# Sparse attention's pair loop: copies out of PSUM put ahead of ScalarE's other work in each step, one scaling moved a step on VectorE, one turning moved ahead on TensorE

## The reference, cut to what matters

```python
def nsa_attention(h, w_in, q_g, kc_g, ks_g, kw_g, pe_k, pe_v, ck_w1, ck_w2, cv_w1, cv_w2, w_out):
    q, kc, vc, ks, vs, kw, vw, gl = jnp.split(h @ w_in, splits, axis=-1)
    q = rmsnorm(heads(q, N_HEADS), q_g)
    q_nope = to_groups(q)
    q_rope = to_groups(partial_rope(q))
    gates = jax.nn.sigmoid(gl)
    k_cmp = rmsnorm(compress(kc_blk, pe_k, ck_w1, ck_w2), kc_g)      # 31 compressed keys
    v_cmp = compress(vc_blk, pe_v, cv_w1, cv_w2)
    ...
        p_c = masked_softmax(einsum(qn, k_cmp) * scale, cmp_end <= pos)
        o_c = einsum(p_c, v_cmp)
        p_s = masked_softmax(einsum(qr, k_g) * scale, mask_s)
        o_s = einsum(p_s, v_g)
        p_w = masked_softmax(einsum(qr, kwb) * scale, mask_w)
        o_w = einsum(p_w, vwb)
        return gt[..., 0:1] * o_c + gt[..., 1:2] * o_s + gt[..., 2:3] * o_w
    return o @ w_out
```

## Time and profile before

| what | value |
|---|---|
| time, median of 3 runs | 2884.02 us (2883.28 to 2886.16) |
| the profiled execution's own time | 2889.93 us |
| its span | 2888.1 us |
| mean granted clock of TensorE | 0.983 |
| PE, DVE, ACT busy | 96%, 57%, 41% of the span |
| NSA's pair loop | about 2237 to 2466 us of the span |
| length of a middle pair, from one start of L1017 to the next | 27.85 us (2286.81 to 2314.66) |

### The profile page before, as it was taken

How to read it: one execution, slowest core, us unless ns; L and a number is a source line. 1 busy time by engine, 2 the same in 40 slices (tenths; PEclk the granted TensorE clock), 3 DMA queues, 4 the chain that set the end, 5 groups by cost and what they waited for, 6 DMA issues and landing times.

```text
span 2888.1 us, 34237 instructions
## 1 busy us (share of the span) xinstructions
PE 2766.0 (96%) x11807; PEld 2092.8 (72%) x11807; DVE 1652.5 (57%) x2288; ACT 1196.0 (41%) x1929; POOL 151.1 (5%) x141
## 2 busy tenths in 40 slices
PE   8999998999989988999989989999997999999999
PEld 6777776888867656888866657888875555788887
DVE  4444426776254755777339955554375787555532
ACT  4333324444243544444236654333244566433321
POOL 0000000000000000000005710000000222000000
PEclk9999999999999999999999999999999999999999
DMA  4222232333322112333321213333333000233322
GB/s 144 76 78 73 73 95 67 100 89 94 95 71 88 52 39 71 95 94 92 92 77 52 66 44 88 94 94 93 91 102 104 15 16 23 73 94 94 94 88 94
DMA packets 419614, 229.26 MB, mean 79 GB/s; under 512 B 7939, under 2 KB 411468, under 8 KB 419404
## 3 DMA queue, kind: packets, MB, share of 16 engines
q1 hardware_dynamic: 418172, 225.18, 26.6%
q10 hardware_dynamic: 1360, 3.02, 0.3%
HBM read 226.07 MB, written 2.10 MB: 79 GB/s over the span
## 4 chain that ended last, share of the span: by engine, by line
PE 83%; DVE 9%; ACT 5%; issue 2%; DMA 1%; POOL 1%; DVEq 0%; ACTq 0%; POOLq 0%; SPq 0%
PE lin L725 21%; PE lin L727 21%; PE lin L726 21%; DVE con_a L2368 2%; PE stat L741 1%; DVE w_lo L1918 1%; PE lin L1025 1%; PE att L870 1%; PE att L834 1%; PE att L833 1%; PE att L835 1%; PE att L986 1%; ACT w_hi L1332 1%; ACT n_pt L1634 1%; PE lin L1048 1%
## 5 line engine op out<-in xcount | busy, mean ns | idle before, releaser
L1918 DVE TENSOR_TENSOR w_lo<-raw,w_hi 128x1024 fp32r<-128x1024 f32 x427 | 527.7, 1236 | 654.0 <-ACT w_hi L1332 639.5
L1332 ACT ACTIVATE w_hi<-raw 128x1024 fp32r<-128x1024 f32 x427 | 452.2, 1059 | 771.1 <-PE lin L727 678.9
L725 PE MATMUL lin<-xh,w_hi 128*128 128x512 f32 x1856 | 741.8, 400 | 4.4 <-DVE w_lo L1918 4.0
L727 PE MATMUL lin<-xh,w_lo 128*128 128x512 f32 x1856 | 733.7, 395 | 0.0
L726 PE MATMUL lin<-xl,w_hi 128*128 128x512 f32 x1856 | 733.7, 395 | 0.0
L725 PEld LDWEIGHTS lin<-xh,w_hi 128*128 128x128 f32 x1856 | 348.5, 188 | 97.0 <-issue 12.0
L726 PEld LDWEIGHTS lin<-xl,w_hi 128*128 128x128 f32 x1856 | 348.5, 188 | 86.9 <-issue 3.4
L727 PEld LDWEIGHTS lin<-xh,w_lo 128*128 128x128 f32 x1856 | 348.3, 188 | 85.3
L726 PE MATMUL lin<-ffn_lo,w_hi 128*128 128x512 f32 x704 | 279.1, 396 | 0.0
L725 PE MATMUL lin<-ffn_hi,w_hi 128*128 128x512 f32 x704 | 279.1, 396 | 0.0
L727 PE MATMUL lin<-ffn_hi,w_lo 128*128 128x512 f32 x704 | 279.1, 396 | 0.0
(11 more groups left out here) (365 smaller groups left out, 3801.8 us busy)
## 6 DMA issues: line engine op xcount, KB each, us to landing
raw<-in_ffn_w_up SPq DMA_DIRECT2D x176, 512.0 KB, 3.8
raw<-in_ffn_w_down SPq DMA_DIRECT2D x64, 512.0 KB, 3.6
raw<-in_a_w_in SPq DMA_DIRECT2D x48, 512.0 KB, 3.8
raw<-in_ffn_w_down SPq DMA_DIRECT2D x32, 384.0 KB, 3.1
raw<-in_conv_w_pw SPq DMA_DIRECT2D x24, 512.0 KB, 3.9
raw<-in_nsa_w_in SPq DMA_DIRECT2D x21, 512.0 KB, 3.8
raw<-in_a_w_out SPq DMA_DIRECT2D x16, 512.0 KB, 3.6
raw<-in_w_kv SPq DMA_DIRECT2D x16, 512.0 KB, 3.9
```

What stands on the lines that cost most here:

```text
L725: pe.matmul(bank, w_hi[s][:, k, :], h, start=start and k == 0, stop=False)
L727: done = pe.matmul(bank, w_lo[s][:, k, :], h, start=False, stop=stop and k == kc - 1)
L1332: act.activation(w_hi[s][:, :, :], raw[s][:, :, :], ACT.Copy).then_inc(hi_done[s], 1)
L1918: dve.tensor_tensor(w_lo[s][:, :, :], raw[s][:, :, :], w_hi[s][:, :, :].bitcast(F32), ALU.subtract).then_inc(lo_done[s], 1)
```

## The change

ScalarE: in every step `place(n)` comes directly behind `exps(n+1)`. It moves ahead of `high_out` in step 1, of `square` in step 2, of `inverse_rms` in step 3 (with the copy `pct`, which stays directly behind it), of `split_next` in step 5 and of `exp_compressed` in step 7. VectorE: `normed_q` moves from step 3 to step 4, directly ahead of `rotated_q`. TensorE: in step 4 `turn(n)` moves ahead of `weigh_compressed` and `weigh(p, 0)`. No instruction is added or taken away.

```diff
@@ TensorE, nsa @@
                         if i == 0 and p:
                             weigh(p - 1, 1, before)
+                        if i == 3 and not last_pair:
+                            head_sums(lin[ub])
+                        turn(n)
                         if i == 4:
                             weigh_compressed(p, own[0])
                             weigh(p, 0, own[0])
-                        if i == 3 and not last_pair:
-                            head_sums(lin[ub])
-                        turn(n)
@@ ScalarE, nsa @@
                             exps(n + 1)
+                        place(n)
                         if i == 1 and p:
                             high_out(p - 1, before)
+                        if i == 3:
+                            act.wait_ge(n_tc, p + 1)
+                            if p:
+                                act.wait_ge(n_pv, 2 * p - 1)
+                            act.activation(pct[:, :], lin[bo][0:2 * NCMP, :], ACT.Copy).then_inc(n_pc, 1)
                         if not last_pair:
...
                                 split_next()
                             if i == 7:
                                 exp_compressed(p + 1)
-                        place(n)
-                        if i == 3:
-                            act.wait_ge(n_tc, p + 1)
-                            if p:
-                                act.wait_ge(n_pv, 2 * p - 1)
-                            act.activation(pct[:, :], lin[bo][0:2 * NCMP, :], ACT.Copy).then_inc(n_pc, 1)
@@ VectorE, nsa @@
                         if not last_pair:
-                            if i == 3:
+                            if i == 4:
                                 normed_q(p + 1, b)
-                            if i == 4:
                                 rotated_q(p + 1)
```

## The result

The changed kernel takes 2908.11 us (median of 4 runs, 2906.65 to 2912.56), the kernel before 2884.13 us (4 runs): a ratio of 1.0083, with a 95% interval of 1.0071 to 1.0095. It is slower by 24.0 us. The direction was forecast, but 24.0 us is more than the 14.5 us predicted, and the time lies above the range. (In the profiles the spans differ by 22.7 us. The loop began 2.8 us later in the kernel before's, 2237.08 against 2234.26 us, which the change has no part in.)

What follows compares the result with a forecast made beforehand. TensorE, 83% of the chain, was taken as the bound, with a mid-pair relay between engines. Six pairs at 2.37 (14.2) + 0.6 first pair - 0.3 last pair = 14.5 us: 2884.0 to 2898.5, range 2890 to 2904.

Steps and rivals of the forecast that it cites:

- pct, turning and q scaling: Fourth and fifth steps: the 0.75 us wait for pct goes; the later q scaling makes the sixth turning wait 0.6.
- square: Behind the third step's copies: head sums 2.30 us late, only some 0.35 us of it on top of att_hi.
- w_hi: Behind the sixth step's copies: exponentials 2.35 us late, so the pair ends about 2.37 late instead of 2.15.
- att_hi: Behind the second step's copies: VectorE's att_lo waits for it, and TensorE's third turning gets 1.95 us of new wait.
- the relay: Engines handing work on mid-pair, TensorE hardly ahead: all moves together make pairs 1 to 6 each 2.37 us longer.
- The second rival: Relay slack absorbs part of the late start; half remains, 1.2 us a pair, 7 us, 2891; chance 0.11.
- so by the row it costs no clock: TensorE's new wait of about 2.2 us keeps clock 1.00, as the last pair's 2.2 us idle did.
- fourth rival: Clock falls in each pair: six times at least 9 us at half rate, 27 us more, 2926; chance 0.06.
- the last pair: att_hi meets VectorE in time and the 1.30 us first-weighing wait goes; 0.3 us of it is kept as gain.
- The third rival: Faster: if att_hi were done before VectorE reaches att_lo, 6.5 us at most gained, 2877.5; chance 0.04.

Runs made afterwards that it cites:

- filled kernel: Changed kernel plus eight unused matmuls in TensorE's third-step wait, pairs 1 to 6; 2900.87 us, ratio 1.0053 against the kernel before.
- e4: Changed kernel with att_hi, the square and the w_hi copy put back ahead of the copies; 2883.45 us, ratio 0.9991 against the kernel before.
- half filled: Changed kernel plus four unused matmuls, not eight, in TensorE's third-step wait, pairs 1 to 6; 2902.77 us, ratio 1.0061 against the kernel before.

## Why the prediction was right and wrong, point by point

**What each move costs in a middle pair**, from the differences of the lengths above, beside the predicted share:

| part | predicted | measured | from |
|---|---|---|---|
| pct, turning and q scaling | -0.75 + 0.60 | -0.33 | 27.83 to 27.50 |
| square | +0.35 on top of att_hi | +0.65 alone | to 28.15 |
| w_hi | +0.22 | +0.25 | to 28.40 |
| att_hi | +1.95 | +1.53 | to 29.93 |
| sum, the relay | +2.37 | +2.10 | |
| clock | 0 | +1.75 mean | 29.98 to 31.73 (means) |

The parts are measured in the order of the rows, and the prediction put att_hi first, so that att_hi and the square are to be compared together: 2.30 predicted, 2.18 measured. att_hi moved alone cost 1.62 us in the one interval that kept its clock (27.82 to 29.44).

**Right: the relay.** Every wait that the prediction named is in the profile near its size: att_lo 2.76 us (2.8), the third turning 2.21 (2.2), the head sums 0.47 (0.6), the sixth turning 0.59 (0.6), no wait for pct. The sum of 2.37 us was 0.27 too large, against 2.10, mostly because pct, turning and q scaling gain 0.33 us a pair and not 0.15. Six times 2.10 is 12.6 us, where 14.2 was forecast. The filled kernel lies 0.53% above the kernel before, some 15 us, close to the 14.5 us forecast, but that is partly luck: some 3 us of it are its last pair, whose clock fell (28.59 us instead of 25.61) and which was to gain 0.3. The second rival, slack that absorbs half, is not borne out.

**Wrong: the clock.** The step that failed is "so by the row it costs no clock". It rested on a single row, the last pair's wait of 2.2 us at 1.00, and gave the fourth rival a chance of 0.06. Waits of that length lowered the clock in six middle pairs of six (changed kernel), in five of six (att_hi alone), and with equal waits and equal busy time even at the very place of the row (exp_compressed left ahead). The row showed one outcome of several, and the rarer one: the same last pair, with the same two waits, had the low clock in the kernel with att_hi moved alone. The rival's mechanism was right and its size wrong: 27 us from 9 us at half rate a pair, where the low stretch lasted some 3 to 7 us and cost 1.75 us in the mean, 10.5 us in all in the profiles and some 8.7 by the medians. The 9 us came from the start of the loop, after 5.00 us of idling, and part of a low stretch here is covered by waits. The Trainium skill ("TensorE: Matmul & The Clock Gate", section "HAM oscillation — how this bites in real kernels") has an example whose waits for DMA, 3 to 5 us long, bring the low clock back in every tile. The trace agrees that it comes back pair after pair, here behind waits of 2.2 us, shorter than that example's; that every such wait brings it, which the prediction read out of it, the runs don't bear out (eleven of twelve middle pairs).

**Wrong: the last pair.** It was to gain 0.3 us. With its wait filled and the clock at 1.00 the interval is 25.40 us, 0.2 less than before, so the relay's part was right there. In the changed kernel the interval is 28.28 us instead of 25.61, 2.7 us longer, with the clock low for some 7 us behind waits of 1.14 and 2.10 us. Part of that can be chance, since the kernel before may fall there in other executions too, as an equal last pair did in another kernel; its one profile doesn't tell. The seven intervals together are 26.1 us longer in the profiles, more than the 24.0 us of the medians: the changed kernel's profiled execution is 4.5 us slower than its median.

**The third rival, faster,** was rightly judged: its condition, att_hi done before VectorE arrives, holds in the kernel with att_hi put back, and even there the square and w_hi make it 0.2% slower. The gain that it promised (6.5 us at most) is 0.33 us a pair when only the useful moves are made, some 2 us.

**Open.** What decides whether the clock falls behind a wait of 2.2 us, and why the interval 3-4 alone is 0.3 us longer than its neighbours in several kernels (27.80 against 27.50 in e4) and lost its clock even half filled. Its sixth turning waits 0.89 us for n_e there instead of 0.59. The trace has where that starts: VectorE begins the q scaling 1.16 us after the maxima ahead of it (in e4 at 2336.27 and 2337.43) where it is 0.87 us in other pairs, and the 0.20 us that it idles are put down to no other engine.

## What to carry to other kernels

A copy that frees a buffer looks urgent, but work that sits in an engine's idle gap should stay in it: put behind an instruction that waits for another engine, it starts when that wait ends and carries its own consumers with it. Follow the moved instruction's reader and what is queued behind that reader; here that walk gave the delay to within 0.3 us of 2.1. Then ask what the new idle time does to TensorE's clock, and don't take one row at the full clock as proof that a wait of its length is free; filling the wait with unused matmuls is a cheap test, and here won back 0.3%.

## What the runs showed of the hardware

- In the changed kernel's third pair the granted clock fell some 1.5 us after TensorE had resumed, not during the wait: 1.00 in the window with the wait, 0.57 in the second window behind it. In the second pair it was low in the first transposes behind the wait.
- It isn't a function of the wait alone: 0.51 in one kernel and 1.00 in another behind equal waits and 0.82 us of work in 3. Behind waits of 2.2 us in middle pairs it fell in 11 of 12 (changed kernel and att_hi moved alone), with about 1.0 us of idle time left in one of six, with a wait of 0.26 us or a filled one in none. A second fall in the changed kernel (interval 3-4) came 2.4 us behind a wait of 0.90 us; waits of 0.89 us in the same place of other kernels had none.
- Work added can shorten a kernel: 8 matmuls in each of six pairs, and 0.3% less time.
- VectorE's product of two tiles took 1.10 us instead of 0.69 beside a GpSimd product of 1.28 us, and its shuffle of one tile 0.73 in both. The Trainium skill ("GPSIMD Engine Reference", section "Key points") has it that GpSimd shares its SBUF interfaces with VectorE, and counts VectorE's instructions with two SBUF inputs among those that contend with it. The trace agrees: the product has two, and the shuffle, which has one and ran beside GpSimd for almost all of its time, was not slower.
